# Norms of a two-block network kernel: root from the sums in PSUM on ScalarE, then reciprocal on VectorE

## The reference, cut to what matters

```python
def rmsnorm(x, g):
    x32 = x.astype(jnp.float32)
    y = x32 * lax.rsqrt(jnp.mean(x32 * x32, axis=-1, keepdims=True) + EPS)   # EPS = 1e-6
    return (y * g.astype(jnp.float32)).astype(x.dtype)
```

```python
def conv_ffn(h, w_up, conv_w, conv_b, w_down):
    u, g = jnp.split(h @ w_up, 2, axis=-1)
    g = causal_dwconv(g, conv_w, conv_b)
    return (jax.nn.silu(g) * u) @ w_down
```

## Time and profile before

| | |
|---|---|
| median of three runs | 1538.54 us (1538.01 to 1543.71) |
| the profiled execution, its own time | 1541.93 us |
| its span | 1540.1 us |
| TensorE (PE) busy | 1477.1 us, 96% |
| weight load (PEld) busy | 1377.7 us, 89% |
| VectorE (DVE) busy | 1006.5 us, 65% |
| ScalarE (ACT) busy | 673.6 us, 44% |
| GpSimd (POOL) busy | 6.8 us |
| mean DMA rate | 178 GB/s |

### The profile page before, as it was taken

How to read it: one execution, slowest core, us unless ns; L and a number is a source line. 1 busy time by engine, 2 the same in 40 slices (tenths; PEclk the granted TensorE clock), 3 DMA queues, 4 the chain that set the end, 5 groups by cost and what they waited for, 6 DMA issues and landing times.

```text
span 1540.1 us, 28698 instructions
## 1 busy us (share of the span) xinstructions
PE 1477.1 (96%) x11886; PEld 1377.7 (89%) x11886; DVE 1006.5 (65%) x1454; ACT 673.6 (44%) x768; POOL 6.8 (0%) x19
## 2 busy tenths in 40 slices
PE   6989999999999899999999999899999999999997
PEld 5987799999877799999787869689999899899997
DVE  5784766666745776666675665657665768666665
ACT  5453544333634643434455443544434433443342
POOL 0000000000000000000000000000000000000000
PEclk9999999999999999999999999999999999999999
DMA  5443645555446345445525566055554554454541
GB/s 232 165 137 136 247 166 190 188 194 191 169 181 251 119 174 208 164 172 208 186 84 189 221 243 251 13 192 184 198 181 173 188 221 166 175 196 178 189 163 55
DMA packets 38815, 274.84 MB, mean 178 GB/s; under 512 B 4432, under 2 KB 5584, under 8 KB 5840
## 3 DMA queue, kind: packets, MB, share of 16 engines
q1 hardware_dynamic: 37296, 264.26, 47.0%
q0 software_dynamic: 720, 6.82, 1.1%
q10 hardware_dynamic: 720, 2.61, 0.4%
HBM read 272.62 MB, written 1.05 MB: 178 GB/s over the span
## 4 chain that ended last, share of the span: by engine, by line
PE 87%; DVE 6%; ACT 3%; DMA 3%; issue 2%; DVEq 0%; SPq 0%; ACTq 0%
PE L L1654 59%; PE D L1654 16%; PE M L1733 2%; DMA raw<-in_units 2%; PE N L1741 2%; ACT whi L483 1%; DVE wlo L918 1%; PE D L2034 1%; DVE arena L995 1%; PE N L2047 1%; PE D L1810 1%; PE D L1777 1%; DMA t<-in_mem 1%; PE N L1799 0%; PE D L1945 0%
## 5 line engine op out<-in xcount | busy, mean ns | idle before, releaser
L1654 PE MATMUL L<-h_hi,whi 128*128 128x256 f32 (+1 forms) x2096 | 613.3, 293 | 28.7 <-DVE wlo L918 15.2
L1654 PE MATMUL L<-h_lo,whi 128*128 128x256 f32 (+1 forms) x2096 | 607.4, 290 | 0.0
L1654 PE MATMUL L<-h_hi,wlo 128*128 128x256 f32 (+1 forms) x2096 | 607.2, 290 | 0.0
L1654 PEld LDWEIGHTS L<-h_hi,whi 128*128 128x128 f32 x2096 | 405.7, 194 | 43.8 <-issue 38.2
L1654 PEld LDWEIGHTS L<-h_lo,whi 128*128 128x128 f32 x2096 | 405.9, 194 | 4.0 <-issue 0.2
L1654 PEld LDWEIGHTS L<-h_hi,wlo 128*128 128x128 f32 x2096 | 405.7, 194 | 4.0
L918 DVE TENSOR_TENSOR wlo<-raw,whi 128x2048 fp32r<-128x2048 f32 x107 | 244.9, 2288 | 129.1 <-ACT whi L483 128.8
L1073 DVE TENSOR_TENSOR wlo<-raw,whi 128x2048 fp32r<-128x2048 f32 x96 | 219.8, 2290 | 111.4 <-ACT whi L609 111.4
L483 ACT ACTIVATE whi<-raw 128x2048 fp32r<-128x2048 f32 x107 | 203.1, 1906 | 132.1 <-PE L L1654 83.9
L1654 PE MATMUL D<-hd_hi,whi 128*128 128x256 f32 x640 | 181.1, 283 | 0.0
L1654 PE MATMUL D<-hd_lo,whi 128*128 128x256 f32 x640 | 181.1, 283 | 0.0
(11 more groups left out here) (285 smaller groups left out, 1801.2 us busy)
## 6 DMA issues: line engine op xcount, KB each, us to landing
raw<-in_units SPq DMA_DIRECT2D x251, 1024.0 KB, 4.9
arena<-in_band POOLq DMA_DIRECT2D x1, 2304.0 KB, 11.4
arena<-in_nax POOLq DMA_DIRECT2D x1, 1536.0 KB, 6.5
t<-in_mem ACTq DMA_DIRECT2D x1, 1024.0 KB, 7.8
x<-in_x ACTq DMA_DIRECT2D x1, 1024.0 KB, 12.3
t<-in_ctx POOLq DMA_DIRECT2D x1, 1024.0 KB, 5.3
arena<-in_ctx POOLq DMA_DIRECT2D x1, 1024.0 KB, 7.3
out<-t SPq DMA_DIRECT2D x8, 128.0 KB, 2.0
```

Source lines behind the costliest of these rows:

```text
L1654: ins = mm(dst, w[a], h[b], start=start and n == 0, stop=stop and n == 2, skip_group_check=True)
```

## The change

At nine of the ten norms ScalarE waits for the sums (`ss_done`) and takes the root of sum/1024 + EPS straight from PSUM, with a 128x1 tile `eps` as the bias and 1/1024 as the scale; VectorE then takes the reciprocal of the root into `rs` (or `rs2`) and raises `rs_done`. The TENSOR_SCALAR is gone. The boundary norm keeps its old order. GpSimd fills `eps` ahead of its first other fills. The calls stand at the same places in each engine's program.

```diff
+        eps = sb("eps", [P, 1])
         @block.gpsimd
         def _(gp):
+            nc.gpsimd.memset(eps[:], EPS).then_inc(R["eps_set"], 1)
             nc.gpsimd.memset(ones[:], 1.0).then_inc(R["ones_set"], 1)
...
-            def root(dst=rs[:]):
+            def root():
+                stats[0] += 1
+                act.wait_ge(R["ss_done"], stats[0])
+                A.activation(var[:], N0[:, 0:T], ACT.Sqrt, bias=eps[:], scale=1.0 / D).then_inc(R["rv_done"], 1)
+
+            def boundary_root():
                 stats[0] += 1
                 act.wait_ge(R["rv_done"], stats[0])
-                A.activation(dst, var[:], ACT.Sqrt).then_inc(R["rs_done"], 1)
+                A.activation(rs[:], var[:], ACT.Sqrt).then_inc(R["rs_done"], 1)
...
             jobs("mk0")
+            act.wait_ge(R["eps_set"], 1)
             root()
...
-            root(rs2)
+            root()
...
-            root()
+            boundary_root()
...
-            def stat(dim=D):
-                dve.wait_ge(R["ss_done"], stats[0] + 1)
+            def stat(dst=rs[:]):
                 stats[0] += 1
-                step(V.tensor_scalar(var[:], N0[:, 0:T], 1.0 / dim, EPS, ALU.mult, ALU.add))
-                sync()
-                V.reciprocal(var[:], var[:]).then_inc(R["rv_done"], 1)
+                dve.wait_ge(R["rv_done"], stats[0])
+                V.reciprocal(dst, var[:]).then_inc(R["rs_done"], 1)
...
-            stat()
+            stat(rs2)
```

More of the change, by code:

```diff
@@ L382, in build @@
         R = {n: sem(n) for n in (
-            "ones_set", "sc_clear", "cc_ready", "rows_clear", "ada_out", "ada_turned", "ctx_hi", "ctx_lo", "sq_done", "ss_done", "rv_done", "rs_done", "t_done",
+            "ones_set", "eps_set", "sc_clear", "cc_ready", "rows_clear", "ada_out", "ada_turned", "ctx_hi", "ctx_lo", "sq_done", "ss_done", "rv_done", "rs_done", "t_done",
             "h_hi_done", "h_lo_done", "rs_turn", "ctx_t", "sg_done", "v1_done", "rs1_done", "x_ready", "mod_ready", "q_silu", "o_sig",
```

## The result

The changed kernel takes 1547.06 us (median of 22 runs, 1542.08 to 1553.14), the kernel before in the same comparison 1542.42 us (22 runs, 1538.01 to 1552.59). The ratio of the times is 1.0033, 95% interval 1.0021 to 1.0044: 5.1 us slower, between 3.2 and 6.8. The forecast was +2.1 us with +1.6 to +2.8 for its own case, and 1537.5 to 1543.8 us as the range. The sign is right, the size is off by more than half, and the time lies outside the range. That the time lies outside is the level: the three runs known then had a median of 1538.54 us, 22 runs have 1542.42, and 5.1 us on top of 1538.54 would be 1543.6, just inside. That the size is off is not: 5.1 is nearly twice the upper end of +2.8.

The account below looks back on a forecast made before the run. TensorE was taken to bound the kernel (87% of the chain of waits). Two held norms cost 2.4 to 3.7 us, minus 0.82 gained elsewhere: +2.1 on 1538.54, so 1540.6 us, range 1537.5 to 1543.8.

Parts of the forecast that it names:

- its own case: Whole kernel: same within noise, +1.6 to +2.8 us, leaning to slower; chance 0.74.
- What is on the path: Full chain waited for at ffn2 and the end; variance and reciprocal hidden at `o_b` and ffn3; TensorE covers five others.
- The two held norms: Norms ahead of `o_b` and ffn3, where ScalarE is held by a modulation row's copy; together +2.4 to +3.7 us.
- The reciprocal behind the held root: At `o_b` and ffn3 the formerly hidden reciprocal comes between root and apply: +1.83 us each.
- The root's 0.47 us: New root from PSUM with a tile bias takes 0.47 us, 0.05 us longer than the old root.
- The gain at ffn2 and at the end: TENSOR_SCALAR leaves the chain at ffn2's and the final norm: gain 0.41 us each, 0.82 together.
- The clock: Behind `o_b` and ffn3 the low stretch stays in place, so later starts net +1.1 and +1.3 us.
- The term of 1.7 us for a low stretch: At `o_b` the 3.4 us at clock 0.50 cost 1.7 us: first unit 7.5 us instead of 5.8.
- The first rival: Longer stops at `o_b` and ffn3 each bring a second low stretch: +6.2 us in all, 1544.7 us; chance 0.12.
- The backlog rival: Earlier VectorE at five covered norms frees TensorE held by late `wlo`: -2.9 us, 1535.6 us; chance 0.1.
- the table load behind the wait: Load comes behind the sums at ffn2 and the final norm, 1.28 us each: +4.7 us, 1543.2 us; chance 0.04.
- time gained ahead of 1020 us: Sign that the forecast is wrong: TensorE gains time in the part of the kernel ahead of 1020 us.

Follow-up runs that it names:

- the fill: Unused filler matmuls in TensorE's stops at `o_b` and ffn3: 3 and 3 in the kernel before, ratio 0.9987; 7 and 6 in the changed kernel, 1.0010.
- the run with the two held norms only: Kernel before with the new order only at the norms ahead of `o_b` and ffn3; ratio to before 1.0027.
- the four experiments without the longer stops and without fill: Change with old order at `o_b`, ffn3 (1.0000); change with root ahead of row calls (0.9986), plus early table load (0.9978); kernel before with root ahead (0.9994).
- the early table: Changed kernel, root ahead of the row calls at `o_b` and ffn3, small root issued early to load the table at three norms; ratio to before 0.9978.

## Why the prediction was wrong, point by point

**What is on the path** was right. The two held norms carry the loss (the run with these alone: 1.0027); the seven others show none (the run with these alone: 1.0000, give or take 2.9 us), and the traces have 0.31 and 0.32 us of gain at two of them.

**The reciprocal behind the held root**, +1.83 us a norm: right. The traces show 3.99 - 2.15 = +1.84 at `o_b` and 2.57 - 0.82 = +1.75 at ffn3, where the new root also overlaps the end of the row's copy.

**The root's 0.47 us**: right, 0.474.

**The gain at ffn2 and at the end**, 0.41 us each: 0.31 and 0.32 measured. The table load, covered before by the variance and the reciprocal, comes into the chain by 0.1 us. I had asked whether the load would move and not what its cover was.

**The clock** is the step that failed. The prediction let the low stretch stay in place, so that a later start would leave less work in it: a first unit of 6.7 us at `o_b` and 6.9 at ffn3, "net +1.1" and "net +1.3". Instead the stretch doubled, to 6.8 us, and the units took 8.00 and 8.53 us (1229.27 to 1237.27 and 1336.95 to 1345.48), where the earlier trace rows and the 1335.76 to 1343.10 of before give 7.48 and 7.34. So the two norms cost +2.37 and +2.94 and not 1.1 and 1.3; even the upper end, 1.83 each, had no added clock in it.

The term of 1.7 us for a low stretch was too large as well. It took 5.8 us for the unit at full clock, 48 matmuls without a pause, but with the fill and a clock of 1.00 the unit takes 6.36, so that the low stretch of before cost 1.1 us at `o_b` and there was less to win back.

The first rival had the doubled stretch with a chance of 0.12 and +6.2 us. Its mechanism is the one the chip showed; it was priced 1.7 us a norm over the upper end, and the runs give 0.5 and 1.1, since part of the doubled stretch falls on the stop itself. The argument that I had set against it, that both of before's stops were followed by one stretch alike, only compared stops of 3.9 and 2.5 us with each other; the new ones, 5.8 and 4.3 (1223.49 to 1229.27 and 1332.67 to 1336.95), were longer than both.

That the doubling is no accident of one trace is seen in the run with the two held norms only, whose stretches are 6.8 us too, in the four experiments without the longer stops and without fill, which have 3.4 at both places, and in the low time of many runs: 40.1 and 42.3 us with the longer stops, 31.5 to 36.2 without them.

What sorts the traces is the longest piece of the stop in which TensorE had nothing at all to do, not even a small product. It was 1.87 us at `o_b` and 1.47 at ffn3 before, 3.72 and 3.22 in the change. Over all twelve traces, pieces of about 0.5 us (the kernels with fill) were followed by no low stretch at these two places, pieces of 1.0 to 2.3 us by one of 3.4 us, and those of 3.2 and 3.7 us by one of 6.8. It is no rule beyond the two places: at ffn2 the kernel before has an idle piece of 1.78 us and a clock of 1.00 behind it. No run lengthened a stop and changed nothing else, and how the length of a stop makes that of the low stretch stays open.

That it is the clock and not something else in the stop is shown by the fill: it leaves the order of the change as it is, takes nothing away that TensorE waits for, and the 0.50 goes from both places, with 4.0 us by the traces and 3.5 by the ratios. The Trainium skill (TensorE: Matmul & The Clock Gate, Part 1) has it that idleness lowers the rate and sustained work restores it; the traces agree, 0.50 in and behind the stops without fill, 1.00 behind those with it.

**The backlog rival** (faster) and **the table load behind the wait**: neither. TensorE's chain behind the first mixer's norm is still 11.51 us of matmuls, as in the earlier trace rows, and the load still starts ahead of the wait's end (1022.55 at ffn2, where the sums end at 1023.7). The prediction also named time gained ahead of 1020 us as a sign that it was wrong, and the changed kernel's trace has 2.6 us there; the five other traces with the same work up to that point, all later, show that this is the spread of single executions.

**The level.** The low time explains most of the spread between runs of one kernel too: over the 22 runs of the change, time and low time correlate at 0.94, with 0.54 us of time for 1 us of low time, and low times from 33.9 to 52.7 us. The three runs of before that the prediction stood on, had two at the lower end of such a spread (1538.01 and 1538.54 us, where 22 runs go from 1538.01 to 1552.59).

Open: the per-run low time differs from kernel to kernel by amounts (31.5 against 36.0 for the early table) that the low stretches at the two norms don't account for. Stretches elsewhere vary from execution to execution: near 505 us all 12 traces have 3.4 to 6.8 us, near 746 ten of them have one, near 1000 three. I have no experiment on them.

## What to carry to other kernels

A step put on a different engine inherits that engine's queue: before moving the first step of a chain to an engine, look at what releases that engine there, since what was hidden beside the hold (here 1.75 us of reciprocal) then comes behind it. The cure here was to issue the root ahead of the calls that hold it, which only pays if the root itself doesn't wait for long: in the old order it held up those calls instead. Where TensorE stands for a chain of small steps, price a longer stop twice, once for the stop and once for the granted clock behind it, and try useless products in the stop. Anything that runs in the shadow of a step to be removed, such as a table load, has to be asked for its new cover.

## What the runs showed of the hardware

A stop lengthened by 1.8 us, with the piece of it in which TensorE did nothing going from 1.87 to 3.72 and from 1.47 to 3.22 us, doubled the low stretch that came with it, from 3.4 to 6.8 us at a granted clock of 0.50, in both places and in both kernels that had the longer stop (the change, and the run with the two held norms only). Some 1.3 us of products into an idle bank in each of two stops made the unchanged kernel 2.0 us faster (0.9987, 0.9975 to 1.0000). A float32 product of 128x128 by 128x256 is recorded as two matmuls, and took 0.44 us for the two. A float32 root of 128x256 out of PSUM with a bias from a tile took 0.474 us on ScalarE, the plain root out of SBUF 0.417; the reciprocal of that shape took 1.75 us on VectorE. Where ScalarE had nothing else to do, the table load for a root began ahead of the end of the root's wait (1022.55 us, sums done at 1023.7).
